# The experts' rows and sums of a two-layer decoder kernel go through DRAM by indirect transfers instead of through one-hot matmuls

## The reference

```
logits = xt @ router                          # 256 x 8, xt = rmsnorm(x)
top_v, top_i = lax.top_k(logits, 2)           # two experts for each token
top_w = softmax(top_v)
gates = sum(one_hot(top_i, 8) * top_w[..., None], axis=1)
for e in range(8):
    out += gates[:, e:e+1] * ((silu(xt @ w_gate[e]) * (xt @ w_up[e])) @ w_down[e])
x = x + out
```

## Time and profile before

| | |
|---|---|
| median of 3 runs | 1308.17 us (1305.84 to 1309.12) |
| the profiled execution | 1308.12 us, of which the span is 1306.2 |
| mean granted clock of TensorE | 0.994 |
| busy, share of the span | PE 97%, VectorE 77%, ScalarE 63%, POOL 2% |
| transferred | 350.6 MB, 268 GB/s over the span |
| weight transfers | 329 of 1024 KB, 4.9 us from issue to landing |
| expert stage | about 508 to 1300 us of the span |

### The profile page before, as it was taken

The page is one execution under the profiler, slowest core; times in us unless marked ns, Lnnn a source line. Parts: engine busy times, 40 slices in busy tenths (PEclk is TensorE's granted clock), DMA queues, the critical chain, the costliest instruction groups (busy, mean ns, idle before and its releaser), DMA issues.

```text
span 1306.2 us, 17280 instructions
## 1 busy us (share of the span) xinstructions
PE 1271.1 (97%) x6144; PEld 1046.0 (80%) x6144; DVE 1011.7 (77%) x1002; ACT 822.0 (63%) x901; POOL 24.0 (2%) x27
## 2 busy tenths in 40 slices
PE   6999999999999998999999999999999999999997
PEld 5877888888888875888888887888888888888885
DVE  4786665444458467889989988989989989989985
ACT  6444364443465455777677677777777777777773
POOL 0130000000000000000000000000000000000000
PEclk9999999999999999999999999999999999999999
DMA  9630045444544333999989999999999999999991
GB/s 376 246 139 24 2 145 183 186 177 182 191 162 161 130 129 119 372 347 365 345 346 365 346 344 363 340 345 370 341 346 361 348 341 367 347 341 369 346 368 63
DMA packets 48793, 350.59 MB, mean 268 GB/s; under 512 B 5424, under 2 KB 5552, under 8 KB 6480
## 3 DMA queue, kind: packets, MB, share of 16 engines
q1 hardware_dynamic: 48720, 349.54, 71.1%
HBM read 348.47 MB, written 1.05 MB: 268 GB/s over the span
## 4 chain that ended last, share of the span: by engine, by line
PE 92%; DVE 4%; ACT 2%; issue 1%; POOL 1%; DMA 0%; SPq 0%; DVEq 0%; ACTq 0%
PE bank L499 27%; PE bank L501 27%; PE bank L500 27%; PE bank L992 1%; PE bank L688 1%; PE bank L714 1%; DVE wlo L1391 1%; PE bank L847 1%; PE bank L696 1%; ACT whi L1084 1%; PE bank L509 1%; PE bank L966 1%; PE bank L968 1%; PE bank L651 1%; PE bank L944 0%
## 5 line engine op out<-in xcount | busy, mean ns | idle before, releaser
L1913 DVE TENSOR_TENSOR wlo<-raw,whi 128x2048 fp32r<-128x2048 f32 x261 | 597.6, 2291 | 81.2 <-ACT whi L1318 78.3
L1318 ACT CAST whi<-raw 128x2048 fp32r<-128x2048 f32 x261 | 499.0, 1912 | 140.6 <-PE bank L501 140.2
L499 PE MATMUL bank<-whi,hT_hi 128*128 128x512 f32 (+1 forms) x1104 | 432.0, 391 | 9.8 <-DVE wlo L1391 7.0
L501 PE MATMUL bank<-whi,hT_lo 128*128 128x512 f32 (+1 forms) x1104 | 429.6, 389 | 0.0
L500 PE MATMUL bank<-wlo,hT_hi 128*128 128x512 f32 (+1 forms) x1104 | 429.0, 389 | 0.0
L499 PEld LDWEIGHTS bank<-whi,hT_hi 128*128 128x128 f32 x1104 | 207.7, 188 | 54.6 <-issue 8.9
L501 PEld LDWEIGHTS bank<-whi,hT_lo 128*128 128x128 f32 x1104 | 207.6, 188 | 43.1
L500 PEld LDWEIGHTS bank<-wlo,hT_hi 128*128 128x128 f32 x1104 | 207.8, 188 | 42.4
L1391 DVE TENSOR_TENSOR wlo<-raw,whi 128x2048 fp32r<-128x2048 f32 x68 | 155.7, 2291 | 100.3 <-ACT whi L1084 99.3
L1084 ACT CAST whi<-raw 128x2048 fp32r<-128x2048 f32 x68 | 129.9, 1912 | 101.2 <-PE bank L501 99.5
L499 PE MATMUL bank<-whi,h_hi 128*128 128x512 f32 x440 | 181.8, 413 | 0.0
(11 more groups left out here) (277 smaller groups left out, 915.7 us busy)
## 6 DMA issues: line engine op xcount, KB each, us to landing
raw<-in_weights SPq DMA_DIRECT2D x329, 1024.0 KB, 4.9
arena<-in_compress SPq DMA_DIRECT2D x1, 1088.0 KB, 14.5
x<-in_x SPq DMA_DIRECT2D x2, 512.0 KB, 5.5
out<-x SPq DMA_DIRECT2D x2, 512.0 KB, 4.0
cst<-in_constants SPq DMA_DIRECT2D x1, 600.0 KB, 10.6
msk_bits<-in_masks SPq DMA_DIRECT2D x1, 288.0 KB, 14.0
sml<-in_small SPq DMA_DIRECT2D x1, 275.0 KB, 3.8
cst<-in_constants SPq DMA_DIRECT2D x1, 64.0 KB, 3.2
```

The lines of the kernel that those rows point to most:

```text
L499: mm(out_, a_hi, b_hi, start=start, stop=False)
L501: return mm(out_, a_lo, b_hi, start=False, stop=stop)
L1318: nc.scalar.copy(whi[:, u % SPLIT, :, :], raw[:, u % RAW, :, :]).then_inc(S["w_hi"], 1)
L1913: V.tensor_tensor(wlo[:, u % SPLIT, :, :], raw[:, u % RAW, :, :], whi[:, u % SPLIT, :, :].bitcast(F32), ALU.subtract).then_inc(S["w_lo"], 1)
```

## The change

A token's rows go through DRAM. VectorE writes the tokens, normalised and with the gain, to `hng` (`normed`), and POOL stores them to a DRAM scratch `tokens`. `positions` works out, for each of a token's two choices, the place in a table (rank x 8 + expert); POOL writes the token's number there by four indirect transfers, and reads the table back as `slot_token` (128 slots by 8 experts). With that it fetches the rows of experts 1 to 7 by indirect transfers (`fetch_rows`) into the two halves of `hn`. TensorE transposes them in chunks 7 and 8 as before, now into banks 3 and 7; `hT_hi` and `hT_lo` are formed straight from the banks. Expert 0 still gets its rows by `gather_rows`.

The sums of experts 0 to 6 are copied to `ybuf` by ScalarE (`store_sums`, in chunk 2 of the next expert) and stored to a DRAM scratch `sums`. After the last of them POOL picks, for each choice of each token, its row (four indirect transfers into `picks`; a choice that isn't there gets a row of zeros), and VectorE adds them to x times the weight (`combine`) in chunks 6 to 9 of expert 7. Expert 7 and the extra rounds still use `combT` and `scatter`.

The expert loop is written out eight times on TensorE, ScalarE and VectorE.

```diff
@@ gpsimd, behind norm(3)
+            pool.wait_ge(S["hn_hi"], NT)
+            nc.gpsimd.dma_start(norm_row, row_d[:, :]).then_inc(S["norm_row"], 16)
...
+            pool.wait_ge(S["table_at"], 1)
+            for w in range(2):
+                for t in range(NT):
+                    nc.gpsimd.indirect_dma_start(table_d[:, :],
+                                                 bass.IndirectOffsetOnAxis(table_at[:, 2 * w + t:2 * w + t + 1], 0),
+                                                 token_id[:, t:t + 1], None).then_inc(S["table_out"], 16)
+            pool.wait_ge(S["table_out"], 64)
+            nc.gpsimd.dma_start(slot_token, table_d[0:NE * CAP, :].rearrange("(p e) o -> p (e o)", e=NE))\
+              .then_inc(S["slot_token"], 16)
+            pool.wait_ge(S["hng"], NT)
+            for t in range(NT):
+                nc.gpsimd.dma_start(tokens_d[t * P:(t + 1) * P, :], hng[:, t, :]).then_inc(S["tokens_out"], 16)
+            pool.wait_ge(S["tokens_out"], 16 * NT)
+            pool.wait_ge(S["slot_token"], 16)
+            def fetch_rows(n):
+                pool.wait_ge(S["xg_psum"], 2 * (n - 1))
+                nc.gpsimd.indirect_dma_start(hn[:, n % 2, :], None, tokens_d[:, :],
+                                             bass.IndirectOffsetOnAxis(slot_token[:, n:n + 1], 0))\
+                  .then_inc(S[("rows_even", "rows_odd")[n % 2]], 16)
+            fetch_rows(1)
+            fetch_rows(2)
+            for e in range(NE - 1):
+                pool.wait_ge(S["y_out"], 2 * (e + 1))
+                nc.gpsimd.dma_start(sums_d[0:Y_NONE, :].rearrange("(p e) d -> e p d", e=NE - 1)[e], ybuf[:, :]).then_inc(S["y_stored"], 16)
+                if e + 3 < NE:
+                    fetch_rows(e + 3)
+            pool.wait_ge(S["sums_at"], 1)
+            pool.wait_ge(S["y_stored"], 16 * (NE - 1))
+            for i in range(4):
+                nc.gpsimd.indirect_dma_start(picks[:, i, :], None, sums_d[:, :],
+                                             bass.IndirectOffsetOnAxis(sums_at[:, i:i + 1], 0))\
+                  .then_inc(S["picks_in"], 16)
@@ tensor, expert()
-                        pe.wait_ge(S["ysb"], e * 2)
+                        pe.wait_ge(S["y_out"], e * 2)
...
-                    if not fresh and c in (SCATTER, SCATTER + 1):
-                        scatter(e - 1, (0, 1) if c == SCATTER else (2, 3))
-                    if c == TURN:
+                    if drain and c == TURN:
...
-                    if not drain and c == GATHER:
-                        gather_rows(e)
                     if not drain and c in (GATHER + 1, GATHER + 2):
-                        gather(e, c - GATHER - 1)
+                        half = c - GATHER - 1
+                        pe.wait_ge(S[("rows_even", "rows_odd")[(e + 1) % 2]], 16 * ((e + 2) // 2))
+                        turn_rows(half, (e + 1) % 2, (3, 7)[half])
...
-            expert(0, U_MOE, 0, fresh=True)
-            with pe.Fori(1, NE - 1, 2) as e:
-                expert(e, U_MOE + EXP_UNITS, 1)
-                expert(e + 1, U_MOE + 2 * EXP_UNITS, 0)
-            expert(NE - 1, U_MOE + (NE - 1) * EXP_UNITS, 1, drain=True)
+            for e in range(NE):
+                expert(e, U_MOE + e * EXP_UNITS, e % 2, fresh=(e == 0), drain=(e == NE - 1))
@@ scalar
+            def store_sums(e):
+                act.wait_ge(S["units_used"], U_MOE + (e + 1) * EXP_UNITS)
+                if e:
+                    act.wait_ge(S["y_stored"], 16 * e)
+                for half in range(2):
+                    nc.scalar.copy(ybuf[:, half * BLK:(half + 1) * BLK], bank[4 + half][:, :]).then_inc(S["y_out"], 1)
@@ vector
+            def positions():
...
+                link(V.tensor_tensor(spot, oh, bc(own, 1, 2), ALU.mult))
...
+                V.tensor_tensor(table_at, aim, dump, ALU.add).then_inc(S["table_at"], 1)
...
+            def normed(t):
+                dve.wait_ge(S["norm_row"], 16)
+                V.scalar_tensor_tensor(hng[:, t, :], x[:, t, :], rstd[:, t:t + 1], norm_row, ALU.mult, ALU.mult)\
+                 .then_inc(S["hng"], 1)
+            def combine(w, t):
+                i = 2 * w + t
+                dve.wait_ge(S["picks_in"], 64)
+                dve.wait_ge(S["x_ready"], X_MOE + i)
+                V.scalar_tensor_tensor(x[:, t, :], picks[:, i, :], w_kept[:, i:i + 1], x[:, t, :], ALU.mult, ALU.add)\
+                 .then_inc(S["x_ready"], 1)
@@ vector, expert(), behind hidden_lower(c - 1)
+                    if fresh and not drain:
+                        if c == 0:
+                            positions()
+                        if c in (1, 2):
+                            normed(c - 1)
+                        if c == TURN + 1:
+                            dve.wait_ge(S["rows_psum"], 2)
+                            prepare(NE - 1, 1)
+                    if drain and not fresh and c in (6, 7, 8, 9):
+                        combine((c - 6) // 2, c % 2)
```

More of the change, by code:

```diff
@@ L129, in constants @@
     c[:, C_FOLD:C_FOLD + NE] = i[:, None] % NE == np.arange(NE)[None, :]
+    for w in range(4):
+        c[:, C_DUMP + w] = NE * CAP + w * P + i
+    for t in range(NT):
+        c[:, C_TOK + t] = (t * P + i).astype(np.int32).view(np.float32)
     for g in range(NG):
@@ L299, in trunk @@
         gslot = sb("gslot", [P, 1])
-        mtab = sb("mtab", [P, 400])
+        ybuf = sb("ybuf", [P, DM])
+        picks = sb("picks", [P, 4, DM])
+        mtab = sb("mtab", [P, 600])
+        tokens_d = nc.dram_tensor("tokens", (SEQ, DM), F32, kind="Internal").ap()
+        sums_d = nc.dram_tensor("sums", (Y_NONE + 1, DM), F32, kind="Internal").ap()
+        table_d = nc.dram_tensor("table", (TABLE, 1), I32, kind="Internal").ap()
+        hng, norm_row, zero_row = picks[:, 0:NT, :], picks[:, 3, :], picks[0:1, 2, :]
         tab_at = [0]
@@ L321, in trunk @@
         ovf = cf(4)
+        spot = cf(2 * 16).rearrange("p (w t n) -> p w t n", w=2, t=2)
+        which, pos, rank_of, fits, aim, kept, w_kept = (cf(4) for _ in range(7))
+        table_at, sums_at = cf(4).bitcast(I32), cf(4).bitcast(I32)
+        tab_zero = cf(TABLE // P).bitcast(I32)
+        slot_token = cf(NE).bitcast(I32)
+        token_id = cst[:, C_TOK:C_TOK + NT].bitcast(I32)
         NAMES = """x_in x_in1 ident_in gain_in const_in tile0 late_in w_hi w_lo units_used x_ready ss rstd root_diag roots_psum roots
@@ L332, in trunk @@
             gla_rstd mixed first_rows logitsT_psum logitsT logits gap gap_exp picked rank route disp
-            combT_psum combT rows_psum rows xg_psum xg cur m_silu m_hact m_h2T_psum m_h2T ysb scat out""".split()
+            combT_psum combT rows_psum rows xg_psum xg cur m_silu m_hact m_h2T_psum m_h2T ysb scat out
+            norm_row zeroed tables_zero hng tokens_out table_at table_out slot_token rows_even rows_odd y_out y_stored sums_at picks_in""".split()
         S = {n: sem(n) for n in NAMES}
@@ L1345, in expert @@
                     if not drain and c in (GATHER + 2, GATHER + 3):
-                        gathered(e, 1 - par, c - GATHER - 2)
+                        fetched(e + 1, c - GATHER - 2)
                     if c >= 2 or not fresh:
                         split_unit(pos_d(c - 2, drain) + SPLIT)
-                    if not drain and c == GATHER:
-                        gathered_rows(e)
                 if drain:
@@ L1353, in expert @@
                     final_sums(e, (e + 1) * EXP_UNITS + U_MOE)
-            gathered_rows(-1)
-            gathered(-1, 0, 0)
-            gathered(-1, 0, 1)
-            expert(0, U_MOE, 0, lambda pos: loads_main(0, U_MOE, pos), fresh=True)
-            with act.Fori(1, NE - 1, 2) as e:
-                expert(e, U_MOE + EXP_UNITS, 1, lambda pos: loads_main(e - 1, U_MOE + EXP_UNITS, pos))
-                expert(e + 1, U_MOE + 2 * EXP_UNITS, 0, lambda pos: loads_main(e - 1, U_MOE + 2 * EXP_UNITS, pos))
-            last = U_MOE + (NE - 1) * EXP_UNITS
-            expert(NE - 1, last, 1, lambda pos: loads_main(0, last, pos), drain=True)
+            gathered_rows(0)
+            gathered(0, 0, 0)
+            gathered(0, 0, 1)
+            for e in range(NE):
+                first = U_MOE + e * EXP_UNITS
+                expert(e, first, e % 2, lambda pos: 16 * ((first + pos) // RAW + 1), fresh=(e == 0), drain=(e == NE - 1))
             act.wait_ge(S["route"], 1)
@@ L1882, in gathered @@
+            def gathered(j, half):
+                dve.wait_ge(S["xg_psum"], half + 1 if j is None else (j + NE - 1) * 2 + half + 1)
                 gc = R_NORM + NK * 3 + 4 * half
@@ L1928, in expert @@
                 for c in range(NCH):
-                    if c == 2 and not fresh:
-                        sums_lower(e - 1)
                     split_unit(pos_g(c, 0, fresh) + SPLIT)
```

186 lines of the change are left out of this document (106 added, 80 removed).

## The result

| | before | after |
|---|---|---|
| median | 1307.14 us (1305.84 to 1309.12, 4 runs) | 1273.39 us (1271.88 to 1275.09, 4 runs) |
| the profiled execution | 1308.12 us | 1275.09 us |
| expert stage, first to last transposes of `hact` | 769.86 us | 735.97 us |
| transferred | 350.6 MB | 361.6 MB |

The ratio is 0.9742 [0.9727, 0.9757]. The forecast started from 1308.1 us, 1.0 more than the kernel before measured beside the changed one.

The account below looks back on a forecast made before the run. The prediction took TensorE's list of matmuls to bound the expert stage. Its terms summed as 1308.1 - 31.6 - 1.2 + 3.8 + 1.2 = 1280.3 us, with a stated range of 1275 to 1292.

Parts of the forecast that it names:

- Term 1: TensorE in the experts: loses scatter halves, `disp` turn and `gather_rows`, keeps the eight transposes; 31.6 us less.
- Term 2: Loop over pairs of experts: unrolling removes TensorE's stalls at two of its ends, 1.2 us less.
- Term 3: VectorE in expert 0: `positions` and two `normed` delay `wlo`, so TensorE loses 3.8 us; bounds 1.5 and 6.
- Term 4: VectorE in expert 7, chunks 6 to 9: four `combine` of 1.2 us cost 1.2 us; bounds 0 and 3.
- Term 7: POOL's row fetches: expert 1's chain takes 6.4 to 29 us of 36 after the second `normed`; hidden.
- rival C: Expert 1's fetch chain late at c=7 of expert 0; 1288 us at 14.5 us a step; chance 0.05.
- Term 8: DMA traffic in the expert stage: 35.65 MB an expert at 379 GB/s, against 351 now; no cost taken.
- A: Transfers become the bound at 377 GB/s, 94.6 us an expert; 1285 to 1290 us; chance 0.12.
- D: Slower than before: transfers sustain only the mean seen, 351 GB/s, giving 1330 us; chance 0.04.
- Rival B: VectorE and POOL's queue obstruct each other in the expert stage, holding up `wlo`: 1300 us, half 1290; chance 0.08.
- Rival E: Added to any outcome: Term 3 stalls lower TensorE's clock, a 3 us dip costing 1.5 us; no separate chance.

Follow-up runs that it names:

- cst_wide: The kernel before with 32 unused bytes behind its constants, so later tensors lie 32 bytes higher: 1302.03 us, ratio 0.9951.
- unrolled: The kernel before with its loop over pairs of experts written out on TensorE, ScalarE and VectorE: 1306.57 us, ratio 0.9984.
- dead_gather: The changed kernel with eight gather matmuls put back in chunk 6 of experts 1 to 6, result unused: 1284.84 us, ratio 0.9813.
- see 5: Expert 0 of the changed kernel: repeated unchanged 1274.99 us; fetches one expert later 1277.02; `positions` ahead of expert 0 1269.32; both edits 1272.28.
- store_x7: The changed kernel with each expert's sums stored seven times, 3.15 MB more an expert: 1296.07 us, ratio 0.9901.
- pad_gone: The changed kernel without the 32-byte `line_pad` ahead of the dense layer's scratch: 1279.29 us, ratio 0.9777.
- h2_moved: The kernel before with 8 unused columns ahead of `h2_hi`, moving it and the tiles behind 32 bytes on: 1304.06 us, ratio 0.9964.
- unrolled_moved: The kernel before with its expert loop written out and `h2_hi`, `h2_lo` moved up 32 bytes: 1301.59 us, ratio 0.9945.
- h2_back: The changed kernel with 8 unused columns ahead of `h2_hi`, moving it 32 bytes on to 169632: 1278.87 us, ratio 0.9778.
- h2_by_64: The changed kernel with 64 bytes put ahead of `h2_hi`, moving it and what follows: 1280.93 us, ratio 0.978.

## Why the prediction fell short

The direction and the mechanism held, a term was missing, and two were too dear. The sum against the two profiled executions; "placement" is compared by cst_wide, which has the kernel before at the changed kernel's addresses (its experts without a loop's end last 97.8 to 97.9):

| term | forecast | measured |
|---|---|---|
| 1 TensorE's list | -31.6 | -31.0: experts 1 to 6 26.6, expert 0 2.5, expert 7 1.9 |
| 2 loop | -1.2 | -1.3 (unrolled; chunks at the loop's ends) |
| 3 `positions`, `normed` | +3.8 | +3.0 |
| 4 `combine` | +1.2 | +0.2 |
| placement | not listed | -4.8 in the stage, -0.9 in the dense layer |
| start of the stage, end | not listed | +2.0 and -0.1 |
| sum | -27.8 | -32.9 (the spans differ by 32.9) |

The +2.0 is 1.25 us ahead of the dense layer's chunks and 0.75 between it and the experts. I don't count the 1.25 as the change's: the first transposes of the dense layer come anywhere between 190.2 and 194.0 us in the profiles of these kernels, which all have the same code ahead of them. The 0.75 is in part a fall of the granted clock at 506 to 510 us, which the profile of the kernel before doesn't have and that of unrolled has; what is left is about 0.4 (159.3 to 159.6 us in the five kernels without the change, 159.5 to 160.0 in the eleven with it), and no run shows what it is.

- **The step that failed** is the listing of the change's parts. The diff widens `cst` by six columns, and the text priced what the columns hold and not where they push the tensors behind them. With 5.7 us for it, known only now, the sum would have been 1274.6, just outside the stated range and 1.2 from the median. The kernel before carried a hint, `line_pad`, 32 bytes with no other use.
- **Term 1** is right to 0.6 us: 0.91 a scatter half, 0.80 the turn and 1.82 the gather at the new placement, where the earlier trace rows gave 0.93, 0.8 and 1.85. dead_gather shows it in the other direction.
- **Term 2** is right; it took the middle of 0.7 to 1.6 from the earlier trace rows.
- **Term 3**: `positions` was priced at 1.9 and cost 1.95; the two `normed` were priced at 0.9 and 1.0 and cost 0.5 each. I held a chunk of VectorE to be 7.5 us with only 0.8 given back; it is 7.28, with starts 0.33 apart behind the small operations where I took their duration of 0.42. On an engine whose starts overlap the ends before them, the term is the distance of starts.
- **Term 4** is the same error: a chunk gives back 8.41 less 7.28, so a `combine` of 1.19 nearly fits, and 0.2 is lost instead of 1.2. Small waits at chunks 6 to 9, which I had named as its sign, aren't there.
- **Term 7 and rival C**: hidden, but the cover was spent to 5 us. I had put two landings behind the second `normed`; the tokens' store also stands behind the table read on POOL's queue, and its landing took 9.6 to 12.8 us (issued 542.9 and 543.5, landed 552.6 and 556.3).
- **Term 8, rivals A and D** are refuted: no chunk of experts 1 to 6 is longer, at 382 GB/s and at 393. A took 377 from a busy share; a share of 0.93 at 351 did not mean a bound at 377. In expert 0 alone weights do come late (see 5), for 0 to 2 us. On D, the Trainium skill ("DMA: Bandwidth & Descriptors", section Specifications) has about 358 GB/s a core from HBM; these windows of 560 us show 382 and 393, and 409 in store_x7. By that figure the kernel would have been slower than before.
- **Rival B** is refuted: `wlo` lasts 2291 ns in the mean over the run, with 57 POOL instructions, and what follows it still starts 2.2 us behind it beside POOL's transfers (522.68 to 524.89, beside the scatter at 522.75). The Trainium skill's rule in "SBUF — State Buffer", section SBUF: two separate sides, holds for GpSimd operations that read SBUF; whether these transfers do, no run here shows.
- **Rival E**: the stall of 2.14 us at the last transposes is again followed by a lower granted clock, 0.59 from 1257 to 1260 (1.2 GHz in most of it), as in the earlier trace rows; and it is 0.58 from 506 to 510, ahead of the stage. But such a stall (2.0 to 2.2 us) stands in all 16 profiles, and the lower clock behind it in 8 only, so the stall alone does not bring it. The new stall of 1.56 us is followed by a clock of 1.00 (525 to 530 us).

## What to carry to other kernels

List what a diff moves, not only what it computes: a wider table shifts every tensor behind it, and here 32 bytes were worth 5.7 us, more than any of the costs that the sum had. A kernel with a placement pad should have the pad tried again with each change of its tensors, and two versions should be compared at the same placement before their difference is put down to the code. A loaded engine's slack is read from distances of starts, and a DMA bound from a run with more traffic, not from a busy share.

## What the runs showed of the hardware

- The pace of a matmul of 512 columns in fp32r hangs on where the tensors lie, its stationary operand or the neighbours of that. Plain chunks by the byte of `h2_hi`: 8.46 us at 169568 (before, pad_gone), 8.41 at 169600 (after, cst_wide; 8.43 in h2_moved and unrolled_moved, with `sg` and `hact` 32 bytes lower), 8.46 at 169632 (h2_back), 8.48 at 169664 (h2_by_64). The difference is in the twelve matmuls of the down product, whose starts, from the second on, are 224 to 236 ns apart in the mean, in a pattern that changes with the address; those of the gate products stay 226 to 228 apart, but for the first few behind the down product at 169632 and 169664 (up to 233 in h2_by_64). Being a multiple of 64 is not the rule, and none was found.
- Beside weights at 382 GB/s, an indirect fetch of 128 rows of 4 KB lands in 11.8 us (median), a plain store of the same size in 6.6 (the tokens' two, issued together, in 9.6 and 12.8), and POOL spends 1.0 to 3.2 us to issue an indirect transfer and about 0.58 on a plain one.
- With a ring of six slots of 1 MB a core's transfers held 393 GB/s over 560 us with TensorE never waiting, and 423 to 425 in windows of 20 us.
- The same program's end differs by 2 us from one execution to the next: behind a stall of 2.0 to 2.2 us of TensorE the granted clock falls to half for about 3.4 us in 8 of 16 profiles (16.5 to 17.1 us to the end) and stays at 1.00 in 8 (14.8 to 15.6). A difference of 2 us in a kernel like this one is therefore read stage by stage.
